# Norm and gate rows read once and spread by products with identity columns, and 512-column gate and up chunks

## What the reference computes

```
mod = silu(c) @ ada_w[l] + ada_b[l]          # (1, 6D): shifts, scales, gates g1, g2
x = layer_norm(ALPHA*x + (1+g1)*mix, ln1_g, ln1_b)     # first network
x = layer_norm(ALPHA*x + (1+g2)*peer(h), ln2_g, ln2_b)
x = x + g1 * rmsnorm(mix, norm_post_mix)               # second network
x = x + g2 * rmsnorm((silu(h @ w_gate) * (h @ w_up)) @ w_down, norm_post_ffn)
```

## Time and profile before

| | |
|---|---|
| median of 3 runs | 2900.17 us (2894.32 to 2902.61) |
| profiled execution | 2893.22 us |
| its span, first to last instruction | 2891.4 us |
| PE busy | 1891.9 us (65%) |
| DVE busy | 1803.3 us (62%) |
| POOL busy | 1071.4 us (37%) |
| ACT busy | 374.6 us (13%) |
| bytes moved | 860.86 MB, of which 538.12 MB by POOL's queue |
| mean granted TensorE clock | 0.799 |

### The profile page before, as it was taken

How to read it: one execution, slowest core, us unless ns; L and a number is a source line. 1 busy time by engine, 2 the same in 40 slices (tenths; PEclk the granted TensorE clock), 3 DMA queues, 4 the chain that set the end, 5 groups by cost and what they waited for, 6 DMA issues and landing times.

```text
span 2891.4 us, 23615 instructions
## 1 busy us (share of the span) xinstructions
PE 1891.9 (65%) x8197; PEld 1332.9 (46%) x8197; DVE 1803.3 (62%) x3281; ACT 374.6 (13%) x830; POOL 1071.4 (37%) x1047
## 2 busy tenths in 40 slices
PE   7889444185644363454364467767188999988998
PEld 4668111064342151142251156643157786477873
DVE  1436999889678889979889986676944200142001
ACT  1311001022102010002011000000014100131000
POOL 1002444577355555755556765465600000000000
PEclk8989556586776685776678788889579999999999
DMA  8366999999999999999999999999860544512443
GB/s 288 111 217 226 399 399 401 369 376 374 371 402 404 400 401 391 336 368 399 399 403 374 339 348 392 368 405 405 323 237 30 189 150 156 189 61 90 157 146 116
DMA packets 359975, 860.86 MB, mean 298 GB/s; under 512 B 23721, under 2 KB 146865, under 8 KB 359729
## 3 DMA queue, kind: packets, MB, share of 16 engines
q0 software_dynamic: 148288, 538.12, 48.4%
q1 hardware_dynamic: 211568, 321.24, 31.9%
HBM read 858.23 MB, written 1.05 MB: 297 GB/s over the span
## 4 chain that ended last, share of the span: by engine, by line
PE 36%; DMA 33%; DVE 14%; issue 11%; POOL 3%; ACT 2%; SPq 0%; DVEq 0%; ACTq 0%
PE bank L927 13%; DMA RING<-in_peer_v,EX 10%; PE bank L415 8%; DMA W<-in_w_ada 6%; PE bank L941 5%; DMA W<-in_ada_w 4%; DMA RING<-in_peer_u,EX 3%; PE bank L424 3%; DMA WORK<-in_peer_u,EX 3%; DMA W<-in_w_up 2%; DVE ACC L1680 2%; POOL RING L1041 2%; PE bank L447 2%; DMA W<-in_w_gate 2%; DMA WORK<-in_peer_v,EX 2%
## 5 line engine op out<-in xcount | busy, mean ns | idle before, releaser
L927 PE MATMUL bank<-HT,W 128*128 128x256 f32 x2112 | 482.0, 392 | 61.6 <-DMA W<-in_w_up 30.3
L927 PEld LDWEIGHTS bank<-HT,W 128*128 128x128 f32 x2112 | 414.8, 197 | 128.6 <-DMA W<-in_w_up 33.9
L1041 POOL DMA_INDIRECT RING<-in_peer_u,EX x343 | 326.4, 952 | 378.8 <-DVE ACC L1662 244.7
L1662 DVE SCALAR_TENSOR_TENSOR ACC<-RING,hrows 128x1024 bf16<-128x1024 f32 x343 | 406.2, 1217 | 79.9 <-DMA RING<-in_peer_u,EX 77.6
L1041 POOL DMA_INDIRECT RING<-in_peer_v,EX x341 | 379.2, 1112 | 206.6 <-DVE hrows L1680 91.5
L447 PE MATMUL bank<-W,CACT 128*32 128x512 f32 x704 | 149.9, 955 | 237.5 <-DMA W<-in_w_ada 135.3
L403 PE MATMUL bank<-consts,XN 128*128 128x128 f32 x208 | 44.6, 397 | 312.4 <-DVE XN L1505 144.6
L415 PE MATMUL bank<-W,HT 128*128 128x256 f32 x992 | 228.7, 394 | 18.6 <-ACT HT L1101 7.4
L941 PE MATMUL bank<-W,WORK 128*128 128x512 f32 x528 | 229.3, 597 | 14.4 <-DVE WORK L2279 14.4
L1041 POOL DMA_INDIRECT WORK<-in_peer_v,EX x171 | 193.7, 1133 | 100.1 <-DVE hrows L1680 39.2
L2279 DVE TENSOR_TENSOR WORK<-WORK,bank 128x256 f32<-128x256 f32 x66 | 27.2, 420 | 321.3 <-ACT WORK L1401 321.3
(11 more groups left out here) (356 smaller groups left out, 2332.1 us busy)
## 6 DMA issues: line engine op xcount, KB each, us to landing
W<-in_w_ada SPq DMA_DIRECT2D x48, 1024.0 KB, 16.4
W<-in_ada_w SPq DMA_DIRECT2D x40, 1024.0 KB, 12.9
W<-in_w_gate SPq DMA_DIRECT2D x33, 1024.0 KB, 5.5
W<-in_w_up SPq DMA_DIRECT2D x33, 1024.0 KB, 5.6
W<-in_w_down SPq DMA_DIRECT2D x33, 1024.0 KB, 5.0
W<-in_w_in SPq DMA_DIRECT2D x32, 1024.0 KB, 13.6
W<-in_peer_wq SPq DMA_DIRECT2D x22, 1024.0 KB, 17.4
W<-in_w_out SPq DMA_DIRECT2D x12, 1024.0 KB, 5.3
```

The costliest lines, as they stand in the source:

```text
L927: mm = pe.matmul(bs[j][:, g * S:(g + 1) * S], w[:, k, j * P:(j + 1) * P], HT[:, k, :], start=(k == 0 and g == 0), stop=(k == DC - 1 and g ...
L1041: gp.indirect_dma_start(SLOT[g % NS], None, rows, bass.IndirectOffsetOnAxis(EX[:, t, k:k + 1], 0))\
L1662: ve.scalar_tensor_tensor(out=JUNK[:, g % 2, :], in0=SLOT[g % NS], scalar=1.0, in1=HB[:, :], op0=ALU.mult, op1=ALU.mult, accum_out=ACTS[:, ...
```

## The change

Ten pairs of rows (both layers) are read once, by ten loads of 8 KB on POOL's queue at the start, into 20 partitions of a new tile `ROWM`, which takes the place of `ROWS`. Where rows are needed, PE makes a product of one identity column, repeated 128 times, with `ROWM`: each partition of the bank then holds the row. This takes two banks for a row. DVE reads them there, in pieces of 512 columns. Gate biases are added by a second product in the same bank as the gate, and the one is added by ACT as it copies the bank out. Only the last norm row pair of `b1` is still broadcast by SP, and that of `b0`'s first norm by POOL at the start. `gate_rows` is one step, not two, so the plan of `stage(0, 0, 1)` has eight places and not nine. Gate and up chunks are 4 rows-blocks by 512 columns, not 8 by 256: still 1 MB, and as many.

```diff
-            def load_rows(a, b):
-
-                load([(ROWS[:, 0, :], a.partition_broadcast(P)), (ROWS[:, 1, :], b.partition_broadcast(P))],
-                     rows_landed, (rows_read, nrows[0]) if nrows[0] else None)
-                nrows[0] += 1
+            def spread_into(b, kind, l, hf, start):
+
+                r = ROW_AT[kind] + l
+                return pe.matmul(b[:, :], ident[0:NROWS, r:r + 1].to_broadcast([NROWS, P]), ROWM[0:NROWS, hf * 512:(hf + 1) * 512],
+                                 start=start, stop=True)
+
+            def spread(name, kind, l):
+
+                for hf in range(2):
+                    b = open_bank((*name, hf), "V")
+                    spread_into(b, kind, l, hf, True).then_inc(filled, 1)
...
                         pe.matmul(b[:, :], const("who")[:, who:who + 1].to_broadcast([P, P]), ROWT[:, half, :],
-                                  start=True, stop=True).then_inc(filled, 1)
+                                  start=True, stop=False)
+                        spread_into(b, ("ada_" if p[0] == "b" else "ada2_") + "12"[(q - 8) // 2], int(p[1]), q % 2, False)\
+                            .then_inc(filled, 1)
...
-                load_rows(d["ln1_g"][l], d["ln1_b"][l])
+                spread(("ln1", p, t, 0), "ln1_g", l)
+                spread(("ln1", p, t, 1), "ln1_b", l)
...
-                for c in range(NF // 2):
+                for f0 in range(0, NF, 4):
+                    nf = min(4, NF - f0)
                     bs = []
                     for g, src in enumerate((wg, wu)):
...
+                        parts = 2 if nf == 4 else 1
+                        for kh in range(parts):
+                            ks = range(kh * DC // parts, (kh + 1) * DC // parts)
+                            w = weight(src[:, ks.start:ks.stop, f0 * P:(f0 + nf) * P])
...
+                            for j in range(nf):
+                                if g == 0 and kh == 0:
+                                    bs.append(open_bank(("gu", p, f0 + j), "V"))
...
             ada("b1", d["ada_w"][1], [0], FIRST, beside=lambda i: gather(0, 0, 0, 10 * i + 64))
-            load_rows(d["norm_post_mix_2"][0], d["norm_post_ffn_2"][0])
+            spread(("post", "c0", 0), "post_mix", 0)
+            spread(("post", "c0", 1), "post_ffn", 0)
...
+            gp.dma_start(HN[:, :], d["ln1_g"][0].partition_broadcast(P)).then_inc(wide_rows, 16)
+            gp.dma_start(ACC[:, :], d["ln1_b"][0].partition_broadcast(P)).then_inc(wide_rows, 16)
...
-            stage(0, 0, 1, {k: [c0] for k in (0, 3, 5, 10, 16, 20, 22, 26, 30)})
+            stage(0, 0, 1, {k: [c0] for k in (0, 3, 8, 14, 18, 20, 24, 29)})
```

More of the change, by code:

```diff
@@ L918, in block2 @@
                     bs = []
                     for g, src in enumerate((wg, wu)):
[L920 to L931, removed]
@@ L1117, in ada @@
                             at = GATES[p, who][(q - 8) // 2]
-                            copy(("ga", p, who, (q - 8) // 2, q % 2), GA[:, at, (q % 2) * 512:(q % 2 + 1) * 512])
+                            name, dst = ("ga", p, who, (q - 8) // 2, q % 2), GA[:, at, (q % 2) * 512:(q % 2 + 1) * 512]
+                            if p[0] == "b":
+                                b = wait_full(act, name)
+                                free(name, A(dst, b[:, :], ACT.Identity, bias=const("one")))
+                            else:
+                                copy(name, dst)
                     yield
@@ L1420, in _ @@
             early = ada("c0", [1, 2], FIRST + SECOND + GATE1 + GATE2)
-            for _ in range(22):
-                next(early)
-            act.wait_ge(mark("gated", "b0"), 1)
             all_of(early)
@@ L1758, in tile1 @@
                 w, n = (t + 1) * 512, (t + 1) * P
-                scaled_rows(f"b{l - 1}", t)
+                scaled_rows("ln2", f"b{l - 1}", t)
                 moments(p, t)
@@ L1870, in tile1 @@
                 yield
-                scaled_rows(p, t)
+                scaled_rows("ln1", p, t)
                 moments(p, t)
@@ L1889, in block1 @@
                 finish_mod(p, p, l, 0, False, 0)
-                def finish_gate(half, bias, s):
-                    wait_empty(ve, *[("ga", p, 0, half, hf) for hf in range(2)])
-                    g = GA[:, gs[half], :]
-                    do(ve.scalar_tensor_tensor(out=g, in0=g, scalar=1.0, in1=bias, op0=ALU.add, op1=ALU.add), s)
                 do(ve.memset(UU[:, :, 0:2], 0.0))
@@ L2023, in block1 @@
                 do(ve.tensor_copy(RT[:, 0:1], RT[:, 0:1]), mark("co", p))
-                finish_gate(0, ROWS[:, 0, :], rows_read)
+                wait_empty(ve, *[("ga", p, 0, 0, hf) for hf in range(2)])
                 for i in (0, 2):
@@ L2046, in gate @@
                 def gate():
-                    finish_gate(1, GA[:, 4, :], mark("gated", p))
+                    wait_empty(ve, *[("ga", p, 0, 1, hf) for hf in range(2)])
                     yield
@@ L2062, in layer_norm @@
                 for t in range(NT):
[L2063 to L2064 removed]
+                    do(ve.scalar_tensor_tensor(out=X[:, t, :], in0=X[:, t, :], scalar=RSD[:, t, 0:1], in1=ACC[:, :],
+                                               op0=ALU.mult, op1=ALU.add))
                 settle()
@@ L2295, in closing @@
             def closing(l, t):
-                scaled_rows(f"b{l}", t)
+                if t == 0:
+                    scaled_rows("ln2", f"b{l}", t)
+                else:
+                    scaled_last(f"b{l}", t)
                 yield
```

107 lines of the change are left out of this document (61 added, 46 removed).

## The result

The changed kernel takes 2934.87 us (median of 4 runs, 2922.11 to 2948.36) beside 2900.25 us for the kernel before; the ratio is 1.0123, 95% interval 1.0072 to 1.0174. It is slower by 35 us where I had forecast 26 us less. The profiled execution has a span of 2927.7 us.

The account below looks back on a forecast made before the run. The prediction took DMA bytes to bound the middle, with DVE close behind, and PE the end. Terms 0 - 1.2 - 11 - 14 - 2 + 2.6 gave -25.6 us, so 2874 us, range 2853 to 2892.

Parts of the forecast that it names:

- Start to 254 us: Kernel start: moved broadcasts cost at most +2.8 us, a shorter SP wait gives at most -3.8; taken as 0.
- `stage(0, 0, 1)`: Stage from 535 to 780 us: cheaper DVE instructions, earlier c0 steps and fewer bytes give -11 us, range -5 to -15.
- the work that follows on PE starts that much sooner, and it is what DVE waits for at the end: In `stage(0, 0, 1)`: c0's steps two rounds sooner start PE's work 10 us sooner, shrinking DVE waits of 14.4 and 5.8 us.
- The tile stages: Four stages with `tile1`: six broadcast pairs fewer give -13 us, with small DVE terms -14, range -6 to -19.
- `c0`'s net: Feed-forward net, 1660 to 2112 us: wider rows -5.4, less bank lookahead +3; term -2 us, range -10 to +9.
- missing are 0 to 9 and 6 to 14, twice each: 12 to 46 us: In `c0`'s net: DVE's picks fall short of PE's 2.75 chunks, so silu waits become 12 to 46 us, not 37.0.
- fewer banks ahead stall the net: Rival for `c0`'s net: DVE waits longer and weights land late, net +53 us, total 2929 us; chance 0.06.
- The -5.4 for wider rows: In `c0`'s net: 2 KB rows cost 0.27 us less per MB than 1 KB rows, -5.4 us over nineteen chunks.
- The end: PE-bound part after 2112 us: added gate and spread products cost +2.6 us, range +1 to +4.
- two more products fill that gap once: In the end part: two added gate products fill PE's wait for ACT, costing +0.9 us, twice.
- DVE as the bound: Rival: DVE limits the kernel, so only removed instructions and half a wait count, about -11 us, 2889 us; chance 0.15.
- Spreads holding banks: Rival: banks filled by spreads stay full until DVE comes, so PE waits at six places, +12 us, 2887; chance 0.06.

Follow-up runs that it names:

- e5: The changed kernel with 256-column chunks in pairs of banks and spreads (the identity-column products) over all 128 rows; 2894.9 us, 1.0010 of the kernel before.
- e6: e5 with POOL's two ln1 broadcasts for b0 held until PE's first product of b0's convolution; 2890.9 us, 0.9997 of the kernel before.
- e10: e6 with c0's attention steps back at the later rounds of the kernel before; 2894.3 us, 0.9987 of the kernel before.
- e15: e13 with 512-column chunks and groups of four banks in l0 and l1 only; 2882.5 us, 0.9961 of the kernel before.
- e7: e6 with twelve 512 KB loads put back into SP's queue in the tile stages, into an unread tile; 2903.3 us, 1.0043 of the kernel before.
- the repeats: The changed kernel run and traced twice more without a change; 1.0125 and 1.0131 of the kernel before.
- e3: The changed kernel with the old 256-column chunks, still in groups of four banks; 2939.2 us, 1.0122 of the kernel before.
- e4: The changed kernel with spreads contracting over all 128 rows, not 20; 2922.0 us, 1.0061 of the kernel before.
- e16: The changed kernel with DVE's c0 gate and up steps at other rounds, mostly two per round; 2899.4 us, 1.0017 of the kernel before.
- e9: e6 with spreads back to contracting over 20 rows; 2912.8 us, 1.0051 of the kernel before.
- e11: e6 with the rows of l0 and l1 as broadcasts again and no spreads there; 2890.8 us, 0.9977 of the kernel before.
- e13: e11 with the later c0 attention rounds of e10; 2884.4 us, 0.9968 of the kernel before.
- e17: e15 with 512-column chunks and groups of four banks in c0 too, and the paired DVE steps of e16; 2906.3 us, 1.0033 of the kernel before.
- e1: The kernel before with only the 512-column chunks and groups of four banks; 2926.7 us, 1.0077 of the kernel before.

## Why the prediction was wrong, point by point

**Start to 254 us: forecast 0, measured +9** (where DVE's layer norm of `b0` starts, 210.0 us and not 201.0). Two steps failed. The broadcasts that POOL now issues cost 5 us in the traces (e5 against e6), above my bound of 2.8. And I never priced the gate products of `b0` with their spreads, where PE is at 1.2 GHz: four records took 3.4 us before and eight take 7.7 now.

**`stage(0, 0, 0)`: -1.2.** Right in size: from DVE's layer norm of `b0` to the end of this stage the change is 1.2 us shorter than before (2.3 in e5, 2.0 in e6). That it came out to the tenth is luck, since one instruction of this size is less than such traces differ by.

**`stage(0, 0, 1)`: forecast -11.** The stage is 6 to 11 us shorter, but that is no gain: the next stage is 9 us longer in the first trace and in e6, and with the old rounds (e10, e15) both come back. The failed step is "the work that follows on PE starts that much sooner, and it is what DVE waits for at the end". PE did start sooner, by 12.5 us in e6, but its weights did not come sooner: its eight chunks ended 2.6 us later, and the wait of 5.8 us for the root behind them became 17.8 (e6). (The view of before from 780 to 1660 us lists that wait of 5.8 us too, since it ends at 780, so "nothing else there is over 1.3 us" misses it.)

**The tile stages: forecast -14.** The price of the bytes was right: 13 us in e7 for six pairs is 2.2 us a pair, in the middle of my 1.6 to 2.8. The six groups of gather waits sum to 94.5 us in e6, and I had written near 95. SP's queue moved 13.6 MB less. The last three stages are 8.3 us shorter in the change and 6.3 in e6. The first one lost as much, by the wait above. In the repeats, e3 and e4 it is 9 to 13 us longer still; slow starts in it do not order that (e3 has none there and takes 246.2 us, e10 has 22 us of them and takes 227.7), so the cause is open.

**`c0`'s net: forecast -2, measured +16.** The step that failed is "missing are 0 to 9 and 6 to 14, twice each: 12 to 46 us": the silu waits are 80 us. I priced 2.75 chunks at 20 to 24 us. But the first chunk of a group stops until the fourth bank is empty, the step that frees it stands 2.6 rounds behind the one that finds the group full, and a group takes 30 us when nothing holds it (e16), most of it behind that point. PE's two longest waits for that bank in the changed kernel (at the first the profile names no releaser):

```profile
1828.93 12.22 PE L939 MATMUL bank<-HT,W 128*128 128x256 f32 x45 [6.40 <-issue]
1870.04 12.15 PE L939 MATMUL bank<-HT,W 128*128 128x256 f32 x45 [6.39 <-DVE WORK L2301]
```

In these two groups there are less than 4 us of slow starts each, and DVE waits 15.5 and 17.1 us at their ends. In the three groups before them PE waits 1.8 us or not at all, slow starts take 20.7, 9.8 and 8.4 us, and DVE waits 16.3, 11.7 and 13.0 us. So both the late banks and the slow starts lengthen the wait, and their shares are open, since no trace has these rounds and no slow starts. With pairs of banks slow starts cost little: the net takes 455.1 to 455.7 us in e9, e10 and e11, with 20 to 23 us of them, and 455.1 and 455.3 in e5 and e6 without. It was the rival "fewer banks ahead stall the net", to which I gave 0.06. That its 2929 us is 6 us from the result is luck: it had the net 53 us longer and the other terms 24 shorter, and took the weights to be late, which they were not. The -5.4 for wider rows has support where nothing waits: from 1680 to 1880 us SP's queue takes 2.64 us per MB in e16 and 2.91 in e6, and e16's net is 6.2 us shorter; but e16 has other rounds as well.

**The end: forecast +2.6, measured +17.7.** I priced spreads at 0.89 us per product, the rate of products with a high clock and 128 rows. That failed where the clock stays at 1.2 GHz: in front of `l1` each gate product and each spread takes 2.07 us, with transposes of 3.43 us behind them where before has 1.91. At 2.4 GHz, from start to start, a product of this sequence takes 1.05 us with 20 rows and 0.86 with 128. The net of `l1` took 154.85 us where it had 152.18. The step "two more products fill that gap once" was wrong as well: with 128 rows the rest is still 3 to 12 us longer than in the three traces of before, and with broadcasts 779.8 to 783.2 us in e11, e13, e15 and e17 (786.0 in e1): PE is the bound there. These stretches follow waits of 3.5 us for weights, and before's own gate products after the same waits show both levels (the first product took 1.6 to 1.9 us, the second 0.9 to 1.7). The Trainium skill ("TensorE: Matmul & The Clock Gate", section "HAM oscillation — how this bites in real kernels") says that waits for DMA between short groups of products return PE to the lower clock; the trace agrees: in front of `l1` sixteen records of L455 take 1.92 us, and behind a wait of 3.50 us for weights eight take 1.93. I should have priced both levels.

**The other rivals.** DVE as the bound: e7 speaks against it, since bytes alone cost 13 us. Spreads holding banks: in all stages PE waits twice at a spread, 12.8 us together, and then waits longer for DVE's rows anyway (20.3 and 22.5 us); DVE's own waits for spread banks are 4.4 us for `scaled_rows`.

## What to carry to other kernels

Ask of every removed wait who profited from it: a stalled consumer stops its gathers, and that is when another queue's weights arrive. When PE fills banks in larger groups, price the next group from the step that empties its last bank, and the group at its full length; emptying them all in one step is worth a trial (e16), but it did not help in e17. Move rows by products only where DMA engines are the bound, contract over all rows, and price them at both clock levels. Trace the kernel before in the same group as the changed one: here a state of PE that came and went between groups is as large as the effects, and the one comparison that would settle it is missing.

## What the runs showed that was not expected

The clock of TensorE stayed at 1.2 GHz through 8 us without a gap when half of the products contracted over 20 rows, in 8 of 14 places, and rose within the same sequence in all ten places with 128.

In 11 of 20 traces PE started one record each 1 to 3 us in stretches, 24 to 105 us of them per trace. Kernels that ran together have them or none has. In ten of these traces the first late record in `c0`'s net starts within 2.1 us of a fetch of instructions (queue q8; 1695.7 and 1696.5 us in the changed kernel), and in the changed kernel's three traces the later ones of the net start 4.7 to 6.7 us behind one. In e1 they do not, and e16 and the kernel before fetch in the same part of the net (1697.0 and 1685.6 us) and start on time. So a fetch is not enough to bring a stretch, and no run isolates what does.
